# Grouped norm of the two scan layers: statistics by position, multiplied on GpSimd during the last samples, with filler matmuls on TensorE

## The reference, cut to what matters

```python
h = h * dA[..., None, None] + dt * outer(x, B)      # 32 heads x 64 x 128 numbers per sample
y = einsum(h, C) + x * d_skip
y = y.reshape(b, L, 2048) * silu(z)
y = rmsnorm(y.reshape(b, L, 8, 256), norm_g.reshape(8, 256)).reshape(b, L, 2048)
return y @ w_out
```

## Time and profile before

| | us |
|---|---|
| median of 3 runs (1956.15 to 1957.5) | 1956.38 |
| the profiled execution, its own time | 1956.49 |
| its span in the trace | 1954.9 |
| mean granted TensorE clock in it | 0.948 of full |

### The profile page before, as it was taken

One profiled execution on the slowest core, in us unless ns is written; L12 is line 12 of the kernel. 1 busy time (PEld: TensorE's weight loads), 2 busy tenths in 40 slices (PEclk: granted clock), 3 DMA queues, 4 the chain that ended last, 5 costly groups with the idle time before them and its releaser, 6 DMA issues.

```text
span 1954.9 us, 35706 instructions
## 1 busy us (share of the span) xinstructions
PE 1774.0 (91%) x13457; PEld 1644.5 (84%) x13457; DVE 1324.6 (68%) x2471; ACT 950.4 (49%) x1722; POOL 498.7 (26%) x419
## 2 busy tenths in 40 slices
PE   6999989999999365899999959999999998999998
PEld 6998759999999233599999959999899875999997
DVE  5989795555575877465557876554799879565455
ACT  4456754453344755255435454533545666445333
POOL 1601401441120334154112015411160060044111
PEclk8999989999999667899999979999999998999999
DMA  6455474655547899765554517554545448465550
GB/s 211 142 181 152 141 230 133 201 183 183 172 169 233 314 398 410 266 207 186 173 172 135 170 55 234 178 183 161 157 139 184 125 137 265 130 200 177 183 175 26
DMA packets 317972, 365.05 MB, mean 187 GB/s; under 512 B 7802, under 2 KB 290978, under 8 KB 317750
## 3 DMA queue, kind: packets, MB, share of 16 engines
q1 hardware_dynamic: 296068, 287.41, 46.7%
q0 software_dynamic: 20560, 74.62, 10.1%
q10 hardware_dynamic: 1216, 1.35, 0.2%
HBM read 340.79 MB, written 23.15 MB: 186 GB/s over the span
## 4 chain that ended last, share of the span: by engine, by line
PE 66%; DVE 18%; ACT 7%; issue 3%; DVEq 3%; DMA 1%; POOLq 1%; POOL 0%; ACTq 0%; SPq 0%
PE G L551 19%; PE G L552 19%; PE G L553 19%; DVE wlo L1681 5%; ACT whi L1061 3%; DVE sums L1994 2%; PE A L997 1%; PE A L512 1%; DVE pg L2056 1%; DVE pg L2054 1%; DVE xbc L1842 1%; ACT raw L1247 1%; PE G L748 1%; DVEq L1844 1%; DVE stx L1986 1%
## 5 line engine op out<-in xcount | busy, mean ns | idle before, releaser
L1681 DVE TENSOR_TENSOR wlo<-raw,whi 128x2048 fp32r<-128x2048 f32 x234 | 547.7, 2341 | 335.8 <-ACT whi L1061 335.6
L1061 ACT ACTIVATE whi<-raw 128x2048 fp32r<-128x2048 f32 x234 | 448.0, 1914 | 560.0 <-PE G L553 555.8
L551 PE MATMUL G<-xH,whi 128*128 128x264 f32 x2112 | 605.0, 286 | 16.9 <-DVE wlo L1681 12.3
L552 PE MATMUL G<-xH,wlo 128*128 128x264 f32 x2112 | 600.1, 284 | 0.0
L553 PE MATMUL G<-xL,whi 128*128 128x264 f32 x2112 | 599.8, 284 | 0.0
L551 PEld LDWEIGHTS G<-xH,whi 128*128 128x128 f32 x2112 | 399.5, 189 | 26.8 <-DVE wlo L1681 13.5
L552 PEld LDWEIGHTS G<-xH,wlo 128*128 128x128 f32 x2112 | 399.7, 189 | 0.1
L553 PEld LDWEIGHTS G<-xL,whi 128*128 128x128 f32 x2112 | 397.8, 188 | 0.0
L551 PE MATMUL G<-aH,whi 128*128 128x264 f32 x1024 | 292.2, 285 | 7.9 <-DVE wlo L1681 7.9
L553 PE MATMUL G<-aL,whi 128*128 128x264 f32 x1024 | 290.7, 284 | 0.0
L552 PE MATMUL G<-aH,wlo 128*128 128x264 f32 x1024 | 290.7, 284 | 0.0
(11 more groups left out here) (440 smaller groups left out, 3032.2 us busy)
## 6 DMA issues: line engine op xcount, KB each, us to landing
raw<-in_mlp_w_up SPq DMA_DIRECT2D x64, 1024.0 KB, 5.3
raw<-in_mlp_w_down SPq DMA_DIRECT2D x64, 1024.0 KB, 5.1
raw<-in_ssd_w_in SPq DMA_DIRECT2D x48, 1024.0 KB, 5.4
pg<-in_cache_k POOLq DMA_DIRECT2D x64, 512.0 KB, 7.3
raw<-in_ssd_w_out SPq DMA_DIRECT2D x16, 1024.0 KB, 6.8
raw<-in_ple_w_gate SPq DMA_DIRECT2D x16, 1024.0 KB, 5.1
raw<-in_moba_w_qkv SPq DMA_DIRECT2D x12, 1024.0 KB, 5.2
pgw<-in_cache_v POOLq DMA_DIRECT2D x24, 512.0 KB, 7.4
```

Of the source, the lines that this page charges most:

```text
L551: mm(o, whi[u % 2][:, k, w], act_h[:, x, :], start=first, stop=False)
L552: mm(o, wlo[u % 2][:, k, w], act_h[:, x, :], start=False, stop=False)
L1061: fn(whi[u % 2][:], raw[(u + 2) % 4][:], ACT.Copy).then_inc(s_hi, 1)
L1681: V.tensor_tensor(wlo[u % 2][:], raw[(u + 2) % 4][:], whi[u % 2][:].bitcast(F32), ALU.subtract).then_inc(s_lo, 1)
```

## The change

1. `norm_part` is turned round: the squares are the stationary operand and `gsel` streams, 8 columns (two halves of 128 positions, so twice as many matmuls). The sums come out by position, 128 partitions by 2x8.
2. ScalarE takes their root after sample 4 instead of 5 (`grt`, 128x16), VectorE the reciprocal between the adds and the contraction of sample 5, TensorE transposes the result to 8x256 behind `spread(5)`, ScalarE copies it out after sample 6, GpSimd splits it into a high and a low part.
3. TensorE broadcasts the rows with 8-row matmuls on these parts (`root_rows`, 4 matmuls of 256 columns for two groups), two calls behind `spread(6)` and two before `spread(7)`. ScalarE copies them out times the gain (`root_copy`), GpSimd multiplies y by them, ScalarE and VectorE make yH and yL of the prompt's columns. The 16 `scaled` steps of VectorE and the 8 broadcasts of before are gone.
4. `warm(o, n)` adds n matmuls whose result nobody reads, to a free PSUM bank: 6 behind the transposes, 18 after the last sample, 8 after the samples' sums. Each has 8 rows and 512 columns.
5. The semaphore `s_finT` at the program's end is replaced by `s_tp0`, which frees a semaphore.

```diff
                 def norm_part(g):
-                    pe.wait_ge(s_gq, GROUPS * q + g + 1)
+                    pe.wait_ge(s_gq, 9 * q + g + 1)
                     for t in range(2):
-                        t_ = mm(bank[2][0:GROUPS, 0:SEQ], gsel[:, g, :], xbc[:, 2 * g + t, 0:SEQ],
-                                start=(g + t == 0), stop=(g == GROUPS - 1 and t == 1), skip_group_check=True)
+                        for c in range(2):
+                            t_ = mm(bank[2][:, c * GROUPS:(c + 1) * GROUPS], xbc[:, 2 * g + t, c * P:(c + 1) * P], gsel[:, g, :],
+                                    start=(g + t + c == 0), stop=(g == GROUPS - 1 and t == 1), skip_group_check=True)
...
+                def root_rows(j):
+                    if j == 0:
+                        pe.wait_ge(s_gq, 9 * (q + 1))
+                    if j >= 2:
+                        pe.wait_ge(s_gc, 4 * q + j - 1)
+                    for e in range(2):
+                        sel, o = hv2["id2"][0:GROUPS, 2 * j + e:2 * j + e + 1].to_broadcast([GROUPS, P]), bank[3 - j % 2][:, e * SEQ:(e + 1) * SEQ]
+                        mm(o, sel, grH, start=(e == 0), stop=False, skip_group_check=True)
+                        t_ = mm(o, sel, grL[:], start=False, stop=(e == 1), skip_group_check=True)
+                    t_.then_inc(s_gb, 1)
+                def warm(o, n):
+                    for _ in range(n):
+                        mm(o, hv2["id2"][0:NB, 0:1].to_broadcast([NB, P]), smp["crH"][:, 0:512], start=True, stop=True)
                 for k in range(1, NB):
                     outer(k, 0)
                     outer(k, 1)
+                    if k == NB - 1:
+                        root_rows(2)
+                        root_rows(3)
                     spread(k)
...
-                pe.wait_ge(s_gs, q + 1)
+                    if k == NB - 3:
+                        pe.wait_ge(s_gs, q + 1)
+                        for c in range(2):
+                            t_ = tr(bank[2][0:GROUPS, SEQ + c * P:SEQ + (c + 1) * P], hv2["grt"][:, c, :], P)
+                        t_.then_inc(s_gv, 1)
+                        warm(bank[3], 6)
+                    if k == NB - 2:
+                        root_rows(0)
+                        root_rows(1)
                 pe.wait_ge(s_add, 2 * NB * (q + 1))
-                for g in range(GROUPS):
-                    t_ = mm(bank[4 + g // 2][:, (g % 2) * SEQ:(g % 2 + 1) * SEQ], ident[0:GROUPS, g:g + 1].to_broadcast([GROUPS, P]),
-                            hv2["grs"][:], start=True, stop=True)
-                    if g % 2:
-                        t_.then_inc(s_gb, 1)
+                warm(bank[4], 18)
                 pe.wait_ge(s_yz, q + 1)
+                pe.wait_ge(s_gc, 4 * (q + 1))
...
                 t_.then_inc(s_gv, 1)
+                warm(bank[4], 8)
```

On ScalarE:

```diff
-                    if k == 5:
-                        act.wait_ge(s_gv, 2 * q + 1)
-                        fn(hv2["grs"][:], bank[2][0:GROUPS, 0:SEQ], ACT.Sqrt, scale=1.0 / 256, bias=epsc[0:GROUPS, 0:1]).then_inc(s_gr, 1)
+                    if k == 4:
+                        act.wait_ge(s_gv, 3 * q + 1)
+                        fn(hv2["grt"][:].rearrange("p c g -> p (c g)"), bank[2][:, 0:2 * GROUPS], ACT.Sqrt, scale=1.0 / 256, bias=epsc[:, 0:1]).then_inc(s_gr, 1)
+                    if k == 6:
+                        act.wait_ge(s_gv, 3 * q + 2)
+                        fn(hv2["grs"][:], bank[2][0:GROUPS, SEQ:2 * SEQ], ACT.Copy).then_inc(s_gr, 1)
+                def root_copy(j):
+                    act.wait_ge(s_gb, 4 * q + j + 1)
+                    for t in range(4):
+                        c = 64 + XT * q + 4 * j + t
+                        f = fn(rooted[:, 4 * j + t, 0:SEQ], bank[3 - j % 2][:, (t // 2) * SEQ:(t // 2 + 1) * SEQ], ACT.Copy,
+                               scale=colB[:, c:c + 1])
+                    f.then_inc(s_gc, 1)
```

On GpSimd, behind the squares:

```diff
+                pool.wait_ge(s_gr, 3 * q + 2)
...
+                for g in range(GROUPS):
+                    if g % 2 == 0:
+                        pool.wait_ge(s_gc, 4 * q + g // 2 + 1)
+                    zz = Z["zs"][:, 2 * g:2 * g + 2, 0:SEQ]
+                    gp.tensor_tensor(zz, zz, rooted[:, 2 * g:2 * g + 2, 0:SEQ], ALU.mult).then_inc(s_zn, 1)
```

On VectorE:

```diff
                     updated(k)
-                    if k == NB - 1:
-                        dve.wait_ge(s_gr, 2 * q + 1)
-                        V.reciprocal(hv2["grs"][:], hv2["grs"][:]).then_inc(s_gs, 1)
+                    if k == 5:
+                        dve.wait_ge(s_gr, 3 * q + 1)
+                        V.reciprocal(hv2["grt"][:], hv2["grt"][:]).then_inc(s_gs, 1)
                     contract(k)
```

More of the change, by code:

```diff
@@ L269, in build_trunk @@
         s_gq = sem("s_gq")
+        s_gc, s_zn = sem("s_gc"), sem("s_zn")
         s_dt7 = sem("s_dt7")
@@ L1044, in _ @@
             final_T(3, A[1], 2)
-            final_T(3, G[last_bank], 1).then_inc(s_finT, 1)
+            final_T(3, G[last_bank], 1).then_inc(s_tp0, 1)
         @block.scalar
@@ L1256, in ssd, with y_high @@
                     sample(k)
-                    if k == 5:
-                        act.wait_ge(s_gv, 2 * q + 1)
-                        fn(hv2["grs"][:], bank[2][0:GROUPS, 0:SEQ], ACT.Sqrt, scale=1.0 / 256, bias=epsc[0:GROUPS, 0:1]).then_inc(s_gr, 1)
-                act.wait_ge(s_gv, 2 * q + 2)
-                fn(hv2["grn"][:].rearrange("p g b -> p (g b)"), bank[3][:, 0:GROUPS * NB], ACT.Sqrt, scale=1.0 / 256,
+                    if k == 4:
[11 more added lines that the diff above has]
+                    f.then_inc(s_gc, 1)
+                def y_high(g):
+                    act.wait_ge(s_zn, GROUPS * q + g + 1)
+                    fn(ysp["yH"][:, 2 * g:2 * g + 2, 0:SEQ], zs[:, 2 * g:2 * g + 2, 0:SEQ], ACT.Copy).then_inc(s_yh, 1)
+                root_copy(0)
+                root_copy(1)
+                y_high(0)
+                y_high(1)
+                root_copy(2)
+                root_copy(3)
+                y_high(2)
+                y_high(3)
+                act.wait_ge(s_gv, 3 * q + 3)
+                fn(hv2["grn"][:].rearrange("p g b -> p (g b)"), bank[2][:, 0:GROUPS * NB], ACT.Sqrt, scale=1.0 / 256,
                    bias=epsc[:, 0:1]).then_inc(s_gr, 1)
-                for g in range(GROUPS):
-                    act.wait_ge(s_yn, GROUPS * q + g + 1)
-                    fn(ysp["yH"][:, 2 * g:2 * g + 2, :], zs[:, 2 * g:2 * g + 2, :], ACT.Copy).then_inc(s_yh, 1)
+                act.wait_ge(s_yn, q + 1)
+                fn(ysp["yH"][:, :, SEQ:T], zs[:, :, SEQ:T], ACT.Copy).then_inc(s_yh, 1)
+                for g in range(4, GROUPS):
+                    y_high(g)
                 def conv_rows(it, u):
@@ L1581, in ssd @@
                     gp.tensor_tensor(Z["xbc"][:, 2 * g:2 * g + 2, 0:SEQ], zz, zz, ALU.mult).then_inc(s_gq, 1)
+                pool.wait_ge(s_gr, 3 * q + 2)
+                one = ones[0:GROUPS, 0:1].to_broadcast([GROUPS, SEQ])
+                gp.tensor_tensor(grH, hv2["grs"][:], one, ALU.mult)
+                pool.drain()
+                gp.tensor_tensor(grL[:], hv2["grs"][:], grH.bitcast(F32), ALU.subtract).then_inc(s_gq, 1)
+                for g in range(GROUPS):
[3 more added lines that the diff above has]
+                    gp.tensor_tensor(zz, zz, rooted[:, 2 * g:2 * g + 2, 0:SEQ], ALU.mult).then_inc(s_zn, 1)
             def moba():
@@ L2031, in ssd @@
                 zsg = zsm.rearrange("p (g e) b -> p g e b", e=2)
-                V.tensor_tensor(zsg, zsg, hv2["grn"][:].unsqueeze(2).to_broadcast([P, GROUPS, 2, NB]), ALU.mult).then_inc(s_yn, 3)
-                for g in range(3, GROUPS):
-                    scaled(g).then_inc(s_yn, 1)
-                    yn_low(g - 3)
-                for g in range(GROUPS - 3, GROUPS):
-                    yn_low(g)
+                V.tensor_tensor(zsg, zsg, hv2["grn"][:].unsqueeze(2).to_broadcast([P, GROUPS, 2, NB]), ALU.mult).then_inc(s_yn, 1)
+                y_low(3)
+                dve.wait_ge(s_yh, 9 * q + 5)
+                V.tensor_tensor(ysp["yL"][:, :, SEQ:T], zsm, ysp["yH"][:, :, SEQ:T].bitcast(F32), ALU.subtract).then_inc(s_mixl, 4)
+                for g in range(4, GROUPS):
+                    y_low(g).then_inc(s_mixl, 1)
                 dve.wait_ge(s_soutA, 16 * 5 * (q + 1))
```

34 lines of the change are left out of this document (15 added, 19 removed).

## The result

| | us |
|---|---|
| after, median of 4 runs (1978.05 to 1987.47) | 1981.47 |
| before, beside it, 4 runs (1955.35 to 1957.5) | 1956.27 |
| ratio, 95% interval | 1.0126 (1.0107 to 1.0144) |
| the profiled execution of after, its own time | 1982.71 |

Slower by 25 us; the forecast was 16. The direction was right, the size was not, and the range (to 1979) missed.

A forecast was written before the change was run, and what follows sets the result against it. VectorE and TensorE were taken to bound the sample loop together, TensorE without reserve, its clock deciding the rest. Terms summed to +7.4 us (layer 0) and +8.8 (layer 3), together +16 on 1956.5: 1972 us, own range 1964 to 1979.

The forecast's parts named there:

- C: Start of the last sample's contraction on VectorE; from it to the first projection matmul took 11.0 us before the change.
- The signs that the prediction named: Clock 0.5 in samples 2 to 4, fillers and first projections; VectorE waits at samples 5 and 6; tail about 11.8 us.
- Three turns (samples 2, 3, 4) feel it: Sample loop: norm sums at lower clock half the time, 1.45 us per turn; +2.9 in layer 0, +4.35 in layer 3.
- ScalarE's root before sample 5: Sample loop: the earlier root delays ScalarE's halves of sample 5, which VectorE wants sooner; +1.4 us, whatever TensorE does.
- Reciprocal: VectorE: 1.66 us ahead of the root's broadcast go; the one on 16 columns in sample 5 costs 0.25 us.
- root rows: The root's broadcast matmuls among samples 6 and 7, partly covered by VectorE's adds: +0.7 us, bounds 0 and 2.
- Products of sample 6 behind fillers: TensorE: these wait for VectorE's reciprocal, two transposes and six fillers; +3.0 us at lower clock, +0.1 at full.
- GpSimd's multiplications at nothing: Eight multiplications of 1.04 us, 8.3 us together, end within the longer tail of 11.8 us: cost 0.
- Tail and first projections: Last contraction's start to first projection 11.8 us against 11.0, +0.8; first projections unchanged with 8-row fillers ahead: 0.
- the first rival: Fillers and turned sums hold full clock from sample 2 to the first projection: -3.5 us per layer, 1949 us; chance 0.21.
- My 8.8 us for a tail at full clock: Last contraction's start to first projection if all fillers run at full clock: 8.8 us, which is -2.2.
- Outside the layers: The rest of the program was to take over what the sample loops lose or gain; no term of its own.

The follow-up runs named there:

- the second profile: The changed kernel run once more, nothing altered, for another profile: 1979.76 us (ratio 1.0103 to the kernel before).
- the run with 128 columns: The changed kernel with its norm sums streaming 128 columns (the 8 selector columns repeated 16 times) instead of 8: 1966.46 us (1.0043).
- the other losses mended: The changed kernel with 128-column norm sums and 128-row fillers (1961.26 us); moving ScalarE's root behind sample 5 there gave 1956.41 us.
- the run with six groups: The changed kernel with 128-column sums, 128-row fillers and ScalarE's root behind sample 5, plus GpSimd multiplying six groups and VectorE two: 1946.61 us (0.9942).
- the kernel with all the other edits: The changed kernel with 128-column sums, 128-row fillers, ScalarE's root behind sample 5, and two groups' multiplications moved from GpSimd to VectorE: 1946.61 us.

## Why the prediction was right or wrong

Per layer, by VectorE's timelines of the two first profiles, in us:

| part | forecast, layers 0 and 3 | measured |
|---|---|---|
| additions of sample 1 to those of sample 5 (the turned sums) | +2.9, +4.35 | +6.4, +5.6 |
| first addition of sample 5 to the second of sample 6 (root, reciprocal on 16 columns, products behind fillers) | +4.65 | +4.4, +3.5 |
| second addition of sample 6 to C (root rows, reciprocal gone) | -0.96 | -0.4, -0.3 |
| tail, C to the first projection | +0.8 | -0.1, +0.7 |
| sample 0 to sample 1 | 0 | 0, +0.3 |
| sum | +7.4, +8.8 | +10.3, +9.7 |
| outside the layers, once | 0 | +6.2 |

The signs that the prediction named came: a clock of 0.5 in parts of the loop and through the tail, a tail of 10.9 and 11.7 us, waits for ScalarE's sample 5 and for the products of sample 6. Two steps failed, and either of them alone would have left the time inside the range: the turns that the prediction counted (4.7 us), and the rest of the program, which it put at nothing (6.2 us).

**Turned sums: mechanism right, count wrong.** "Three turns (samples 2, 3, 4) feel it" is the step that failed. The sums of sample 4 stand ahead of the products of sample 5, so four turns feel it. The turns to samples 2, 3, 4 and 5 grew by 0.6, 1.5, 2.0 and 2.3 us in layer 0 and by 0.3, 1.6, 1.7 and 2.0 in layer 3. The fourth is 4.3 us of the 4.7 that the sum lacked (0.5 of it ScalarE's, see below). The price of a turn, 7.45 us with "half of the time at each level", was near: the turns to samples 3 and 4 took 7.9 to 8.0, with the lower clock for 62% of the loop of layer 0. That share is partly luck: in the second profile the same loop had a clock of 0.81 in layer 0 and 0.70 in layer 3, and the four turns lost 2.6 and 7.1 us:

```profile
242.00:264.00 22.00, 22.00 (x99) 17.32 (x98) 17.98 (x104) 10.75 (x34) 0.00 (x0) 0.81 0.66 191
1628.00:1654.00 26.00, 26.00 (x103) 20.09 (x102) 18.09 (x106) 11.56 (x38) 0.00 (x0) 0.70 0.57 166
```

That the sums act through the clock and not through their own length is shown by the run with 128 columns: longer by 0.1 us, and the turns are back.

**ScalarE's root before sample 5** (+1.4): alone in the kernel before it costs VectorE 1.5 us, as forecast. In after VectorE's waits are 1.9 us, but TensorE's products of sample 5 end at 269.65 and 271.96, only 0.5 us before ScalarE's halves (270.15 and 272.49), and in layer 3 they end after these. So the term is mostly counted twice there, with the turned sums, and "this stays" was wrong. What the sum lacked is that the root's place delays the reciprocal too, and with it TensorE and its clock: 3.4 us in layer 0 with the other losses mended.

**Reciprocal** (0.25 for 16 columns): 0.24 us. Its gain of 1.66, taken from the chain, arrives only by 0.4 and 0.3: VectorE's second addition of sample 7 now waits 0.37 us for its products, and C waits 0.94 us for `spread(7)`, which stands behind the root rows of groups 4 to 7. I had put 0.7 us on the root rows; these two waits are 1.3 us in layer 0.

**Products of sample 6 behind fillers** (+3.0): VectorE waits 3.2 us for them in layer 0 and 1.7 in layer 3. Most of them run at the lower clock, as forecast; the six fillers ahead of them take 2.4 us in layer 0 and only 1.6 in layer 3.

**GpSimd's multiplications at nothing: wrong, but hidden here.** VectorE's step of 0.29 us takes 1.20 beside them, about the length of one multiplication (5.04/4 = 1.26 us, not the 1.04 of the earlier trace rows). In after the 18 fillers hold the samples' sums until 296.93 anyway, so the loss shows only once they are mended; then it is 1.5 us of the tail, as the run with six groups shows. By the Trainium skill, "Trainium Architecture — The Big Picture", section "What this means for kernel authors", VectorE and GpSimd share a pair of ports under an exclusive lock; the rows agree, and VectorE's contraction, whose second operand is in PSUM, took 3.6 us with and without GpSimd beside it.

**Tail and first projections**: near the forecast (-0.1 and +0.7 for +0.8), with the clock at 0.50. The Trainium skill's "TensorE: Matmul & The Clock Gate", section "What's actually happening", has the clock follow how busy the engine is; here it stood at 0.50 with 4.90 of 4.90 and 7.50 of 7.50 us busy on 8-row fillers and the first projections, and at 1.00 with 2.56 of 3.90 us busy behind 128-row fillers. The measurement decides: in this kernel being busy was not enough. So the first rival (the fillers hold the clock) fell for 8-row fillers, and the run with 128-row fillers shows its clock, though not its time. My 8.8 us for a tail at full clock was right only with GpSimd out of the way (8.6), in the kernel with all the other edits.

**Outside the layers: put at nothing.** The prediction let the loops' losses be "taken over by the whole rest of the program", and its range left nothing for a rest that changes. The first pair of profiles differs there by 6.2 us: 3.1 in the stage between the layers, where two profiles of the kernel before differ by 3.6 themselves, and 2.6 behind the last one, where both profiles of after lose them. 1.5 us of these are a stretch of lower clock in a place that the edit doesn't touch; whether the change brings it about stays open.

## What to carry to other kernels

A filler is worth its time only if rows of the same kernel show the full clock on matmuls of its shape; fillers of 8 rows cost 2.4 to 3.9 us per layer and raised nothing, and fillers of 128 rows gained some 5 us in the kernel before but none in the layers of the changed one. A matmul made cheaper by streaming fewer columns can slow its neighbours through the clock, all those that stand behind it: count them in the engine's order. Where weight loads bound it, repeated columns are nearly free (0.1 us here). A wait belongs to the source that came last, whatever name the profile puts on it. Before work goes to GpSimd, look at which of VectorE's SBUF-only steps run beside it, and before a small activation goes ahead in ScalarE's order, look at who is waiting for what stands behind it.

## What the runs showed of the hardware that was not expected

- VectorE's 128x128 steps on SBUF took up to 1.25 us beside GpSimd's multiplications, 0.29 alone; contractions with an operand in PSUM did not change (3.6 us for sixteen).
- GpSimd's 128x512 product of two tiles took 1.26 us, the square of one tile 1.04.
- 128-row fillers behind 2.42 us of idle TensorE took 2.91 us for six, behind 0.99 us of idle 1.64 (granted clock 0.50 and 1.00).
- Profiles of one kernel differ by up to 3.6 us in a stage that is the same, with the clock: between the scan layers the kernel before took 1315.4 us at a mean of 0.95 and 1319.0 and 1318.6 at 0.94.
- A pause of TensorE of 1.81 us was followed by 0.50 in after and by 1.00 in before, in every profile of either.
